# Weights laid out on the host in runs of 8 KB, and a beginning that works by k-tile

## The reference

```python
silu_c, silu_cc = jax.nn.silu(c), jax.nn.silu(c_ctx)
mod_lat = (silu_c @ ada_w[i] + ada_b[i])[:, None, :]
sh1, sc1, g1, sh2, sc2, g2 = jnp.split(mod_lat, N_MOD, axis=-1)
h_lat = rms_norm(x, norm_mix_g[i]) * (1 + sc1) + sh1
h_ctx = rms_norm(ctx, norm_mix_g[i]) * (1 + csc1) + csh1
q_l, k_l, v_l = project_qkv(h_lat, attn_w_qkv[j], ...)      # 2048 x 3072 weights
k_c, v_c = project_kv(h_ctx, attn_w_qkv[j][:, D_MODEL:], ...)
```

## Time and profile before

| | us |
|---|---|
| median of three runs | 2005.79 |
| lowest, highest | 2003.09, 2006.72 |
| the profiled execution | 2005.52 |
| its span | 2003.6 |
| PE busy in the span | 1965.9 (98%) |
| DVE, ACT busy | 1391.5, 969.3 |

### The profile page before, as it was taken

One profiled execution on the slowest core, in us unless ns is written; L12 is line 12 of the kernel. 1 busy time (PEld: TensorE's weight loads), 2 busy tenths in 40 slices (PEclk: granted clock), 3 DMA queues, 4 the chain that ended last, 5 costly groups with the idle time before them and its releaser, 6 DMA issues.

```text
span 2003.6 us, 24992 instructions
## 1 busy us (share of the span) xinstructions
PE 1965.9 (98%) x10188; PEld 1609.5 (80%) x10188; DVE 1391.5 (69%) x1424; ACT 969.3 (48%) x1265; POOL 110.9 (6%) x196
## 2 busy tenths in 40 slices
PE   6999989999999999999999999999999999999998
PEld 4677756778888888888888888788888888888886
DVE  3666998889867787788888675766666455555556
ACT  6432565455544455544444464555554454444444
POOL 1111001000000000000000000000000000000000
PEclk9999999999999999999999999999999999999999
DMA  9998768779989899799999626577776566555653
GB/s 359 338 378 319 277 257 297 272 252 323 353 293 348 313 360 364 262 367 363 355 395 383 219 85 193 175 252 253 257 251 220 187 192 210 189 192 198 218 190 126
DMA packets 152261, 542.80 MB, mean 271 GB/s; under 512 B 9393, under 2 KB 10577, under 8 KB 114641
## 3 DMA queue, kind: packets, MB, share of 16 engines
q1 hardware_dynamic: 119312, 335.77, 47.9%
q0 software_dynamic: 31744, 201.34, 27.1%
q10 hardware_dynamic: 1090, 4.09, 0.5%
HBM read 535.91 MB, written 2.10 MB: 269 GB/s over the span
## 4 chain that ended last, share of the span: by engine, by line
PE 94%; DVE 3%; ACT 1%; DMA 1%; issue 1%; POOL 0%; ACTq 0%; DVEq 0%; POOLq 0%
PE ps L2098 13%; PE ps L2036 12%; PE ps L2032 12%; PE ps L2035 11%; PE ps L2096 11%; PE ps L2099 6%; PE ps L1848 6%; PE ps L2095 6%; PE ps L1849 5%; PE ps L1850 5%; PE ps L2257 1%; PE ps L1913 1%; PE ps L2204 1%; DMA spare<-in_ada_w 1%; PE ps L2242 1%
## 5 line engine op out<-in xcount | busy, mean ns | idle before, releaser
L1201 DVE TENSOR_TENSOR w_lo<-raw,w_hi 128x1024 fp32r<-128x1024 f32 x616 | 749.5, 1223 | 467.9 <-ACT w_hi L727 467.6
L727 ACT ACTIVATE w_hi<-raw 128x1024 fp32r<-128x1024 f32 x616 | 649.4, 1059 | 845.7 <-PE ps L2036 345.8
L2098 PE MATMUL ps<-hh,w_hi 128*128 128x512 f32 x1088 | 427.5, 398 | 1.1 <-DVE hh L1627 1.1
L2032 PE MATMUL ps<-w_hi,hh 128*128 128x512 f32 x992 | 385.9, 389 | 0.0
L2036 PE MATMUL ps<-w_hi,hh 128*128 128x512 f32 x992 | 385.9, 389 | 0.0
L2035 PE MATMUL ps<-w_lo,hh 128*128 128x512 f32 x992 | 385.9, 389 | 0.0
L2096 PE MATMUL ps<-hh,w_hi 128*128 128x512 f32 x960 | 379.9, 396 | 0.0
L2099 PE MATMUL ps<-hh,w_lo 128*128 128x256 f32 x1088 | 302.9, 278 | 0.0
L2095 PE MATMUL ps<-hh,w_lo 128*128 128x256 f32 x960 | 267.5, 279 | 0.0
L2099 PEld LDWEIGHTS ps<-hh,w_lo 128*128 128x128 f32 x1088 | 205.7, 189 | 40.9
L2035 PEld LDWEIGHTS ps<-w_lo,hh 128*128 128x128 f32 x992 | 186.2, 188 | 38.9
(11 more groups left out here) (252 smaller groups left out, 1620.4 us busy)
## 6 DMA issues: line engine op xcount, KB each, us to landing
raw<-in_mlp_w SPq DMA_DIRECT2D x256, 1024.0 KB, 5.3
ada_raw<-in_ada_w POOLq DMA_DIRECT2D x151, 1024.0 KB, 6.2
spare<-in_ada_w POOLq DMA_DIRECT2D x29, 1024.0 KB, 6.6
raw<-in_attn_w_qkv SPq DMA_DIRECT2D x24, 1024.0 KB, 10.1
raw<-in_attn_w_o SPq DMA_DIRECT2D x16, 1024.0 KB, 5.7
raw<-in_fourier_w_o SPq DMA_DIRECT2D x16, 1024.0 KB, 5.1
g_row<-in_ada_w POOLq DMA_DIRECT2D x12, 1024.0 KB, 9.0
g_row<-gate_rows SPq DMA_DIRECT2D x48, 64.0 KB, 5.2
```

The lines of the kernel that those rows point to most:

```text
L727: act.activation(w_slot(s)[0], raw[:, piece % RAW, s % 2, :], ACT.Copy).then_inc(hi_ready, 1)
L1201: nc.vector.tensor_tensor(lo, raw[:, s // 2 % RAW, s % 2, :], hi.bitcast(F32), ALU.subtract).then_inc(lo_ready, 1)
L2032: ins = mm(bank_of(tt, nb), h_hi[:, k % KT, tok], hi[:, cols], start=start, stop=False)
L2098: mm(both, w_hi[:, s % SPLIT, w], hh[:, k, :, :], start=(k == 0), stop=False, skip_group_check=True)
```

## The change

The host lays the weights out anew: each piece of 1 MB is contiguous in HBM in the order in which it stands in SBUF, so each of the 128 partitions gets one run of 8 KB, where it got four of 2 KB (QKV pieces from the seventh on, `w_o`, Fourier map, `w1`), two of 4 KB (first six QKV pieces), or, in the first modulation pieces, eight of 1 KB. The loads of `w2`, of x, of the context and of the later modulation vectors stay.

The first modulation pieces are cut otherwise: pieces 0 and 1 have shift and scale of k-tile 0, pieces 2 and 3 those of k-tile 1. Each goes to its own PSUM bank (6 and 5), is copied, turned into columns and added by itself. On PE the first half (k-tile 0) of products 0 to 3 stands ahead of the transposes 4 and 5 of x. SyncE issues the first weight piece when modulation piece 0 has landed, the second one when piece 2 has.

The core of the diff:

```diff
-        sp.wait_ge(ada_in[start_slot(1)], 16)
         for p in range(24):
-            if p < 6:
-                load_first(p)
-            else:
-                load_columns(p, wqkv_v[p // 6, column_block(p)])
+            if p < 2:
+                sp.wait_ge(ada_in[start_slot(2 * p)], 16)
+            load_packed(p, w_qkv[p])
...
-            if n < 8:
-                dst, src = ring(start_slot(n)).rearrange("p (k c) -> p k c", k=8), first_v[n // 4, n % 4 // 2, n % 2]
-            else:
-                dst, src = ring(start_slot(n)).rearrange("p (k c) -> p k c", k=4), start_v[n // 8, n % 8 // 4, n % 4]
-            pool.dma_start(dst, src).then_inc(ada_in[start_slot(n)], 16)
+            pool.dma_start(ring(start_slot(n)), ada_start[n]).then_inc(ada_in[start_slot(n)], 16)
...
+        def first_rows(kt):
+            act.wait_ge(ada_mm, 2 * kt + 2)
+            act.activation(ada_rows[:, kt * T:(kt + 1) * T], ps[:, 6 - kt, kt * T:(kt + 1) * T],
+                           ACT.Copy).then_inc((early_rows, rows_copied)[kt], 1)
+        def shape_first(kt):
+            act.wait_ge((a_first, a_ready)[kt], 1)
+            act.wait_ge(x_T_out, 1)
+            act.activation(xT[:, kt, :], xT[:, kt, :], ACT.Identity, bias=mod_col[:, kt:kt + 1],
+                           scale=a_col[:, 0, kt:kt + 1]).then_inc(mod_done, 1)
+            shaped[0] += 1
+            act.wait_ge(mod_done, shaped[0])
+            act.activation(h_hi[:, kt, :], xT[:, kt, :], ACT.Copy).then_inc((first_hi, hhi_ready)[kt], 1)
...
+        first_rows(0)
+        split_hi(0)
         x_out(0)
+        shape_first(0)
+        first_rows(1)
         x_out(1)
-        rows_out(0)
-        split_hi(0)
-        shape(0, 0)
         split_hi(1)
         x_out(2)
         x_out(3)
+        shape_first(1)
         x_out(4)
         x_out(5)
         split_hi(2)
...
+        def take_first_k(kt):
+            dve.wait_ge((col_first, col_mm)[kt], 1)
+            if kt == 0:
+                dve.wait_ge(vec_ready, 3)
+            at = slice(kt, 17 + kt, 16)
+            nc.vector.tensor_tensor(mod_col[:, at], ps[:, 6 - kt, 4 * kt:4 * kt + 4:2], bias_col[:, at],
+                                    ALU.add).then_inc((first_mods, start_mods)[kt], 1)
+            dve.wait_ge((first_mods, start_mods)[kt], 1)
+            nc.vector.scalar_tensor_tensor(a_col[:, 0, kt:kt + 1], mod_col[:, 16 + kt:17 + kt], 1.0,
+                                           misc[:, V_MIX + kt:V_MIX + kt + 1], ALU.add, ALU.mult).then_inc((a_first, a_ready)[kt], 1)
+        def lower_first(kt):
+            dve.wait_ge((first_hi, hhi_ready)[kt], 1)
+            nc.vector.tensor_tensor(h_lo[:, kt, :], xT[:, kt, :], h_hi[:, kt, :].bitcast(F32),
+                                    ALU.subtract).then_inc((first_h, h_ready)[kt], 1)
...
-        take_first(0, 0)
+        take_first_k(0)
         split_lo(0)
-        lower(0, 0)
+        lower_first(0)
+        take_first_k(1)
         split_lo(1)
+        lower_first(1)
         take_first(0, 1)
...
-        def product(r):
+        def product(r, part=None):
...
+            if part == 0:
+                pe.wait_ge(first_h, 1)
+            else:
+                pe.wait_ge(h_ready, 2 * c + 1 + tt // 2)
...
+        first_cols(0, (0, 1))
         first_piece(2)
         turn_input(0)
         turn_input(1)
         first_piece(3)
         turn_input(2)
-        first_cols(0)
-        for i in range(3, 6):
-            turn_input(i)
+        turn_input(3)
+        first_cols(0, (2, 3))
...
+        for r in range(4):
+            product(r, 0)
+        turn_input(4)
         for r in range(77):
-            product(r)
+            product(r, 1 if r < 4 else None)
+            if r == 0:
+                pe.wait_ge(start_mods, 2)
+                turn_input(5)
...
+def by_columns(w):
+    return w.reshape(4, 4, P, -1, 512).transpose(3, 0, 2, 1, 4).reshape(-1, 4, P, D)
+def start_pieces(w):
+    rows = w[:, 0:2 * D]
+    first = rows.reshape(2, 8, P, 2, 8, 2, P).transpose(4, 5, 0, 2, 1, 3, 6)[0:2].reshape(8, P, D)
+    later = rows.reshape(4, 4, P, 2, 4, 512).transpose(4, 3, 0, 2, 1, 5)[1:4].reshape(24, P, D)
+    return np.ascontiguousarray(np.concatenate([first, later]))
```

More of the change, by code:

```diff
@@ L371, in layer_block @@
     x_in = sem("x_in")
+    first_hi = sem("first_hi")
+    first_h = sem("first_h")
+    first_mods = sem("first_mods")
+    a_first = sem("a_first")
+    col_first = sem("col_first")
+    early_rows = sem("early_rows")
     ctx_rows_in = sem("ctx_rows_in")
@@ L555, in load_piece, with load_packed @@
             sp.dma_start(raw[:, piece % RAW, :, :], src).then_inc(raw_in[piece % RAW], 16)
[L557 to L568, removed]
+        def load_packed(piece, src):
+            load_piece(piece, src.rearrange("p (h n) -> p h n", h=2))
         def load_bias(v):
@@ L1853, in tile_out @@
             return ps[:, bank0 + j // 2, (j % 2) * T:(j % 2 + 1) * T]
-        def product(r):
+        def product(r, part=None):
             p, cb, tt = product_at(r)
             c = r // 16
-            if r < 5:
+            if part == 1:
+                pass
+            elif r < 5:
                 pe.wait_ge(x_T_out, (1, 2, 3, 4, 7)[r])
@@ L1869, in product @@
             n = kts.stop - kts.start
-            for k in range(n):
+            for k in range(n) if part is None else (part,):
                 sl, b = (2 * p + k // 2, k % 2) if n == 4 else (2 * p + k, cb % 2)
@@ L1886, in first_piece, with first_cols @@
                 j = 32 * (k % 4)
-                ins = mm(ps[j:j + 32, 6, m * T:(m + 1) * T], silu[:, 8 * q + k, :], w[:, k, :], start=(q == 0 and k < 4),
+                ins = mm(ps[j:j + 32, 6 - (n // 2 == 1), t * T:(t + 1) * T], silu[:, 8 * q + k, :], w[:, k, :], start=(q == 0 and k < 4),
                          stop=(q == 1 and k >= 4), skip_group_check=True)
             ins.then_inc(ada_mm, 1)
-        def first_cols(c):
-            pe.wait_ge(rows_copied, c + 1)
-            pe.wait_ge(pick_ready, 2)
-            for f in range(4):
-                ins = mm(ps[:, 6, 2 * f:2 * f + 2], ada_rows[:, f * P:(f + 1) * P], pick_first[:, :], start=True, stop=True)
-            ins.then_inc(col_mm, 1)
+        def first_cols(c, part=(0, 1, 2, 3)):
+            if part == (0, 1):
+                pe.wait_ge(early_rows, 1)
+                pe.wait_ge(pick_ready, 2)
+            else:
+                pe.wait_ge(rows_copied, c + 1)
+            for f in part:
+                ins = mm(ps[:, 6 - (c == 0 and f > 1), 2 * f:2 * f + 2], ada_rows[:, f * P:(f + 1) * P], pick_first[:, :], start=True,
+                         stop=True)
+            ins.then_inc(col_first if part == (0, 1) else col_mm, 1)
         def ada_piece(n):
@@ L2427, with qkv_pieces @@
         "attn_k_norm_g", "attn_w_o", "fourier_w_o", "mlp_w1", "mlp_w2", "final_norm_g"]
+def by_columns(w):
+    return w.reshape(4, 4, P, -1, 512).transpose(3, 0, 2, 1, 4).reshape(-1, 4, P, D)
+def qkv_pieces(w):
+    first = w.reshape(8, 2, P, 3, NC).transpose(0, 3, 2, 1, 4)[0:2].reshape(6, P, D)
+    columns = by_columns(w)
+    return np.concatenate([first, np.stack([columns[column_block(p), p // 6] for p in range(6, 24)])])
+def start_pieces(w):
[3 more added lines that the diff above has]
+    return np.ascontiguousarray(np.concatenate([first, later]))
 def kernel(**inputs):
@@ L2444 @@
             a = a[:, TOKENS]
+        if name == "attn_w_qkv":
+            a = qkv_pieces(a[0])
+        if name in ("attn_w_o", "fourier_w_o"):
+            a = by_columns(a[0])
+        if name == "mlp_w1":
+            a = _np.stack([by_columns(a[0]), by_columns(a[1])])
         a = _np.ascontiguousarray(a)
```

31 lines of the change are left out of this document (14 added, 17 removed).

## The result

| | before | changed |
|---|---|---|
| median, us | 2005.75 | 2009.09 |
| lowest, highest (17 runs each) | 2003.09, 2007.70 | 2007.88, 2010.84 |
| the profiled execution | 2005.52 | 2008.30 |
| its span | 2003.6 | 2006.5 |

The changed kernel is slower: 1.0018 of the time of before, 95% interval 1.0012 to 1.0024. A second measurement gave 1.0016 (1.0007 to 1.0025). The forecast was 2004.5, a gain of 1.0 us, in 2001.0 to 2007.3. What was measured is a loss of 3.3 us, outside that range.

The account below looks back on a forecast made before the run. TensorE, busy 1965.9 of 2003.6 us, bounds the kernel, with ScalarE also full from 39.4 to 48.6. First product at 28.2 and slice 3 at 36.0 give 1.0 us: 2005.52 - 1.0 = 2004.5 us, range 2001.0 to 2007.3.

Parts of the forecast that it names:

- What bounds the kernel: TensorE is busy 1965.9 of 2003.6 us, so any gain or loss arises before about 50 us and is carried on.
- The sum: Whole kernel: 1.0 us gained; vectors at 18.6 give 2.4, at 21.1 give -0.1; with the clock -1.1 to +3.4.
- The layout's rate: First modulation pieces: 8 KB runs in place of 1 KB raise the transfer rate from 340 to 412 GB/s.
- What larger packets do to their neighbours: x and vectors share engines with 8 KB packets: x's second half takes 5.1 us, not 4.1; squares start at 12.4.
- The pair of 0.636: One packet of x plus one 8 KB packet of GpSimd's pieces take 0.636 us on an engine, before 0.51.
- The vectors: Biases and gains behind x land at 18.6 us without weight packets between, up to 21.1 with; 20.0 taken.
- the vectors come last: Slower rival, 18%: weight packets go before the vectors, which land at 21.1; first product 30.8, time 2007.1 us.
- the neighbours are not slowed: Rival, 17%: x and the vectors keep their times beside 8 KB rows; 3.0 us won, time 2002.5 us.
- PE up to the first product: TensorE's work from the vectors' transposes on takes 8.2 us without a wait; first product at 28.2, against 29.29.
- From there to slice 3: ScalarE's round of weight slice 3 begins at 36.0, 1.0 us earlier; TensorE stands about 2 us before it.
- The clock: TensorE's rise from 1.2 to 2.4 GHz: 2 us later in the work loses 1 us, sooner wins 1 us.
- gains what PE gains: Rival, 8%: ScalarE's copies fit TensorE's order better, so TensorE's 2.8 us arrive at 48.61; time 2002.7 us.

Follow-up runs that it names:

- x first: GpSimd's first issue held until c, c_ctx and the identity have landed: changed kernel 2003.81 us; program of before with the new layout 2003.20 and 2003.02 us.
- the second (28.68): Second trace of the kernel before, with nothing changed; measured 2005.86 us, ratio 1.0001.
- nine traces above: Traces in the order by k-tile: the changed kernel twice and seven of its variants in 1 KB runs, waits or ScalarE order; medians 2002.94 to 2009.09 us.
- identity matmuls of no use: Changed kernel with GpSimd held for c, SyncE's late wait, and 30, 6 and 7 useless matmuls while TensorE would stand still; 2005.57 us, ratio 1.0003.
- the run where they began at 6.83: Changed kernel with GpSimd held for c, SyncE's late wait, and 44, 12 and 12 useless matmuls; 2008.98 us, ratio 1.0021.

## Why the prediction was wrong, point by point

- **What bounds the kernel** held: 2.4 of the 2.9 us arise before 57 us; the rest comes in steps of some tenths, nearly all before 250 us.
- **The sum** was 1.0 us of gain; the first product was to be 1.1 us earlier (28.2) and is 2.5 us later (31.78). Between the two profiled executions the account closes: 3.6 us more up to the first product, 0.2 more from there to slice 3 and 0.4 less behind it (19.66 for 20.04) turn 1.0 of gain into the 2.4 of loss before 57 us.
- **The layout's rate** held: from 4 to 24 us the queues moved 412 GB/s, 372 before, and q0's turns grew to 7.1 KB (0.79 MB in 112 packets). The Trainium skill's preference for packets of at most 4096 B on the GpSimd path (DMA: Bandwidth & Descriptors, SWDGE vs HWDGE vs iDMA) does not show in these rows. The program of before with the layout and x first gains 2.5 us; how much of it is the rate's is not shown.
- **What larger packets do to their neighbours** is the step that failed: the time at which x lands, forecast at 12.4 and measured at 16.48. I wrote that "the second half of x is 8 packets on each engine: 4.1 us now, 5.1 then", and so left x's first half alone with the engines, as in the trace of before. But there it was alone because GpSimd took 0.92 us for an issue and its first packet came 2.8 us after x's. With 8 KB runs q0 is ahead of x by 1.4 us, and both halves take turns: 16 packets in pairs of 0.636 are 10.2 us from 4.06 us on, which is 14.2; the third queue's 63 packets of 0.31 us over 16 engines add 1.2, and the last packet of x ends at 15.4. The pair of 0.636 was right; the number of pairs was 16 and not 8. What I missed is that the issue gets shorter with fewer runs. That this sets the order is shown by the runs on either side of it: with 1 KB runs q0's first packet is behind x's again (5.55, x at 12.33), and with 8 KB runs and the issue held back too (7.33, x at 10.56).
- **The vectors**: they came 5.9 us behind x (16.48 and 22.39), where I had 6.4 without and up to 8.9 with weight packets between, and took 7.8 (12.2 and 20.0). The weight piece took most of its turns beside x, not beside the vectors. That the vectors would be there last was wrong in the changed kernel, if by little: x's chain ends 0.67 us behind them.
- **The rival "the vectors come last"** has the nearest time (2007.1), and its sign came true (vectors after 21.0, PE at 1.2 GHz up to the products), but its mechanism was only partly there: SyncE's earlier issue cost 1.2 us of the first product. The rest begins with the queue that I had taken as unchanged; with GpSimd held and SyncE's waits as they are, the vectors are used at 17.19. **The rival "the neighbours are not slowed"** fell with x at 16.48.
- **PE up to the first product**: 8.2 us counted, 9.39 measured (22.39 to 31.78). The last root at 23.32 delayed the row copy (0.67 us of idle PE), and the two pieces took 1.93 and 1.91 us where I had 1.52 for the second.
- **From there to slice 3**: 7.8 us forecast, 7.98 measured, and PE's 1.87 us of waiting were as forecast. What was wrong is the comparison: I took 29.2 as the point at which both orders are level, from a trace with a slow stretch in just that place, which the matmuls of 0.43 us at 33.20 showed. Without it the old order needs 6.17 us, so the level point lies 1.8 us ahead of the old order's first product: at 27.5 by the first trace (29.29), at 26.9 by the second (28.68). The two runs with the first pieces in 1 KB are the test: first product at 28.2 to 28.4, and 1.0006 and 1.0007 of the time of before, not 1 us less. So even with x on time the forecast gain of 1.0 us did not come; a half-clock stretch of 1.6 us behind slice 3, in both traces, is part of that.
- **The clock**: full at the first product and behind it, as forecast, but only from about 30.3 us on, behind both pieces, where I had it inside the second.
- **The rival "gains what PE gains"** fell with the 1.86 to 1.88 us of waiting in all traces of this order.

Open stays why in the new order a half-clock stretch follows the wait for slice 3 in five of the nine traces above (* in the last column) and not in the others, and what the layout alone is worth once x is first.

## What to carry to other kernels

The layout that made the transfers cheaper also made their issue shorter (0.56 us for 0.92), and so moved them ahead of x: ask for each transfer not only how fast it is but which one it now overtakes, and hold back the queue that can wait. Here one wait ahead of GpSimd's first issue turned 3.3 us of loss into 1.7 of gain in the new order of work (2009.09 and 2003.81), and 4.7 of loss into 2.5 of gain in the old one (2010.17 and 2003.20). An earlier first product was worth nothing by itself here, where the work taken from ahead of it stood behind it; compare the place where the engines are full again. And a level point read off one trace must be cleared of what belongs to that execution.

## What the runs showed of the hardware

- A GpSimd issue of 1 MB took 0.92 us with 1024 runs and 0.56 us with 128. Its first packet came 1.4 us behind the start of the issue where no packet of x was under way yet (1.25 and 2.62) and 4.1 us behind it where x had filled the engines (3.28 and 7.33).
- Queues took turns by packets: from 7.2 to 10.8 us 107 packets of x stood against 112 of GpSimd's with 8 KB runs (0.75 and 0.79 MB), and before 134 against 140 with 1 KB runs (0.81 and 0.57 MB).
- The granted clock was 1.00 from 12.6 to 29.3 us in the changed kernel while the 16 matmuls of a piece took 1.93 us, which is the 1.2 GHz level (1.07 at the other); only later stretches show in the granted clock (0.82, 0.83, and 0.50 for 5.3 us). The identity matmuls of no use (two instructions each) stood 0.21 us apart from 3.41 to 9.49 us and 0.11 from then on; in the run where they began at 6.83 the change came at 10.83.
